# Expert weights in one 2 MB transfer per slot, with the middle layer's columns reordered

## The reference

```python
gu = xe @ w_gu[e]               # (32, 1024) @ (1024, 4096)
ga, up = split(gu, 2)           # 2048 columns each
y = (silu(ga) * up) @ w_down[e] # (32, 2048) @ (2048, 1024)
```

## Time and profile before

| | |
|---|---|
| time, three runs | 1652.12 us median (1649.69 to 1652.52) |
| span of the profiled execution | 1646.8 us (the profile gives its span alone; the timed runs lie 2.9 to 5.7 us above it) |
| busy share of the span | PE 79%, PEld 46%, DVE 22%, ACT 18%, POOL 4% |
| moved from memory | 499.67 MB, mean 304 GB/s |
| expert weights | 256 gate/up and 128 down transfers of 1 MB |

### The profile page before, as it was taken

One profiled execution on the slowest core, in us unless ns is written; L12 is line 12 of the kernel. 1 busy time (PEld: TensorE's weight loads), 2 busy tenths in 40 slices (PEclk: granted clock), 3 DMA queues, 4 the chain that ended last, 5 costly groups with the idle time before them and its releaser, 6 DMA issues.

```text
span 1646.8 us, 17841 instructions
## 1 busy us (share of the span) xinstructions
PE 1296.5 (79%) x7421; PEld 764.9 (46%) x7421; DVE 360.7 (22%) x552; ACT 289.1 (18%) x388; POOL 58.5 (4%) x37
## 2 busy tenths in 40 slices
PE   6999999999998989986566676577567576567665
PEld 5898778999776646532122122123122122122212
DVE  4653454555427142300000000000000000000001
ACT  4443443333344132200000000000000000000001
POOL 1000000000064000000000000000000000000000
PEclk9998999999998789987887877877887877777787
DMA  9553344555543008399999999999999999999996
GB/s 342 208 175 132 111 145 154 184 175 205 198 160 103 0 0 335 150 372 414 420 416 414 420 416 415 419 417 416 418 417 415 417 418 415 417 419 415 416 420 275
DMA packets 128030, 501.36 MB, mean 304 GB/s; under 512 B 7870, under 2 KB 32644, under 8 KB 94964
## 3 DMA queue, kind: packets, MB, share of 16 engines
q1 hardware_dynamic: 126628, 495.60, 76.1%
q0 software_dynamic: 1360, 5.15, 0.9%
HBM read 499.67 MB, written 1.05 MB: 304 GB/s over the span
## 4 chain that ended last, share of the span: by engine, by line
issue 58%; PE 35%; DVE 3%; ACT 1%; DMA 1%; SPq 0%; POOL 0%; POOLq 0%; ACTq 0%; DVEq 0%
PE psA L525 10%; PE psA L514 9%; PE psB L703 4%; PE psA L880 2%; DMA arena<-in_w_in_dram 1%; PE psA L574 1%; PE psA L919 1%; PE psB L681 1%; PE psA L712 1%; DVE arena L1602 1%; PE psB L630 1%; PE psB L631 0%; PE psB L838 0%; DVE arena L1639 0%; PE psB L787 0%
## 5 line engine op out<-in xcount | busy, mean ns | idle before, releaser
L987 PE MATMUL psB<-arena 128*32 128x512 f32 x2048 | 327.5, 772 | 238.2 <-DMA arena<-in_expert_w_gu_dram 237.5
L987 PEld LDWEIGHTS psB<-arena 128*32 128x32 f32 x2048 | 63.4, 125 | 476.8 <-DMA arena<-in_expert_w_gu_dram 356.2
L1405 DVE TENSOR_TENSOR split_r<-arena,split_r 128x2048 fp32r<-128x2048 f32 x65 | 148.9, 2291 | 183.2 <-ACT split_r L1056 183.2
L525 PE MATMUL psA<-hT_r,split_r 128*128 128x256 f32 x1536 | 185.9, 283 | 1.0 <-ACT hT_r L1065 1.0
L525 PEld LDWEIGHTS psA<-hT_r,split_r 128*128 128x128 f32 x1536 | 184.8, 192 | 2.0 <-ACT hT_r L1065 1.2
L1056 ACT CAST split_r<-arena 128x2048 fp32r<-128x2048 f32 x73 | 138.9, 1905 | 229.7 <-PE psA L525 113.3
L514 PE MATMUL psA<-split_r,hT_r 128*128 128x512 f32 x720 | 170.6, 397 | 5.2 <-ACT split_r L1056 3.0
L1312 ACT ACTIVATE arena<-psB 128x512 f32<-128x512 f32 x16 | 9.6, 597 | 878.3 <-PE psB L987 878.3
L1014 PE MATMUL psB<-arena,vs_b 128*32 128x512 f32 x1024 | 149.1, 737 | 16.3 <-DMA arena<-in_expert_w_down_dram 16.2
L514 PEld LDWEIGHTS psA<-split_r,hT_r 128*128 128x128 f32 x720 | 136.7, 192 | 36.3 <-issue 3.9
L964 PE MATMUL psB<-sb_b,xn_b 128*128 (+1 forms) x544 | 108.6, 377 | 12.3 <-ACT vs_b L1314 12.3
(11 more groups left out here) (313 smaller groups left out, 868.7 us busy)
## 6 DMA issues: line engine op xcount, KB each, us to landing
arena<-in_expert_w_gu_dram SPq DMA_DIRECT2D x256, 1024.0 KB, 25.5
arena<-in_expert_w_down_dram SPq DMA_DIRECT2D x128, 1024.0 KB, 20.6
arena<-in_w_in_dram SPq DMA_DIRECT2D x36, 1024.0 KB, 7.4
arena<-in_w_gate_dram SPq DMA_DIRECT2D x11, 1024.0 KB, 5.5
arena<-in_w_up_dram SPq DMA_DIRECT2D x11, 1024.0 KB, 8.1
arena<-in_w_down_dram SPq DMA_DIRECT2D x10, 1024.0 KB, 5.9
arena<-in_w_out_dram SPq DMA_DIRECT2D x8, 1024.0 KB, 6.3
arena<-in_ca_wkv_dram SPq DMA_DIRECT2D x4, 1024.0 KB, 6.4
```

What stands on the lines that cost most here:

```text
L525: ins = pe.matmul(psA[:, 2 * pair + b, f * TOK:(f + 1) * TOK], w[:, k, f * P:(f + 1) * P], x[:, k, :], start=(j == 0 and k == 0), stop=(j ...
L987: ins = pe.matmul(psB[32 * j:32 * j + 32, o, :], XC[:, k, :], w[:, o * EFF + j * NC:o * EFF + (j + 1) * NC], start=(k == 0), stop=(k == GU ...
L1405: v.tensor_tensor(W_LO[n % 2].rearrange("p (k n) -> p k n", **shape), view, W_HI[n % 2].bitcast(F32).rearrange("p (k n) -> p k n", **shape ...
```

## The change

One transfer now fills a slot, for both kinds of weights, and adds 16 to the slot's semaphore, so PE's wait counts 16 in place of 32. For gate/up each partition gets its whole row of 4096 columns. For down each partition gets four neighbouring rows of `w_down`, 16 KB that lie together in memory: partition p holds rows 512 j + 4 p + c. Block c of `HTE` must then hold the columns 4 p + c of the middle layer in place of 128 c + p; DVE's multiply writes `HE` in that order, reading `SL` and the bank straight on and writing with a stride of 128 elements.

```diff
                     s = x_slot[x_place(n)]
-                    for h in range(2):
-                        dst = s[:, h * HALF:(h + 1) * HALF]
-                        if j < GU_SLOTS:
-                            w = A["expert_w_gu_2"][0].rearrange("e k n -> (e k) n")
-                            src = w[bass.ds(e * (BODY * D) + (q * D + j * P), P), h * HALF:(h + 1) * HALF]
-                        else:
-                            w = A["expert_w_down_2"][0].rearrange("e (k p) n -> (e k) p n", p=P)
-                            src = w[bass.ds(e * (BODY * EFF // P) + (q * EFF // P + (j - GU_SLOTS) * 4 + 2 * h), 2), :, :].rearrange("k p n -> p k n")
-                            dst = dst.rearrange("p (k n) -> p k n", k=2)
-                        sp.dma_start(dst, src).then_inc(sig(f"expert_loaded{x_place(n)}"), 16)
+                    if j < GU_SLOTS:
+                        w = A["expert_w_gu_2"][0].rearrange("e k n -> (e k) n")
+                        src = w[bass.ds(e * (BODY * D) + (q * D + j * P), P), :]
+                    else:
+                        w = A["expert_w_down_2"][0].rearrange("e (r k) n -> (e r) (k n)", k=4)
+                        src = w[bass.ds(e * (BODY * EFF // 4) + (q * EFF // 4 + (j - GU_SLOTS) * P), P), :]
+                    sp.dma_start(s, src).then_inc(sig(f"expert_loaded{x_place(n)}"), 16)
...
-                        pe.wait_ge(sig(f"expert_loaded{x_place(n)}"), e * (32 * B_SLOTS // X_SLOTS) + 32 * (n // X_SLOTS + 1))
+                        pe.wait_ge(sig(f"expert_loaded{x_place(n)}"), e * (16 * B_SLOTS // X_SLOTS) + 16 * (n // X_SLOTS + 1))
...
-                    v.tensor_tensor(HE, SL, psB[:, 1, :], ALU.mult).then_inc(sig("e_he"), 1)
+                    v.tensor_tensor(HE.rearrange("p (c n) -> p n c", c=4), SL.rearrange("p (n c) -> p n c", c=4),
+                                    psB[:, 1, :].rearrange("p (n c) -> p n c", c=4), ALU.mult).then_inc(sig("e_he"), 1)
```

## The result

The changed kernel takes 1622.6 us (median of 4 runs, 1619.7 to 1628.9), the kernel before in the same comparison 1650.9 (4 runs, 1646.2 to 1652.5): ratio 0.9846, 95% interval 0.9815 to 0.9878, or 20 to 31 us saved. The profiled execution took 1621.85 us with a span of 1619.8, 2.05 us less; the 2.9 to 5.7 us at "Time and profile before" set the span beside other executions, and hold their spread too.

A forecast was written before the change was run, and what follows sets the result against it. The expert stage was taken as a DMA-bound stream of 2 MB slots. Saving 75 ns on 120 gate/up slots and 195 ns on 64 down slots gives 9.0 + 12.5 = 21.5 us, so 1652.1 becomes 1630.6 us, range 1622 to 1645.

The forecast's parts named there:

- What bounds the kernel: Expert stage: a DMA-bound stream of 2 MB slots, 4.990 us per gate/up slot and 5.110 us per down slot.
- (d): Expert stream: 120 gate/up and 64 down slots, 925.8 us, are the path; the change takes 21.5 us off.
- (a): Gate/up slots: 16 data packets per engine become 8, 60 ns less a slot.
- (b): Down slots: 32 data packets per engine become 8, 180 ns less a slot.
- the price of a packet: Weight transfers: each data packet costs an engine 7.5 ns, or 9.2 ns through the outer two points.
- (c): Each slot: one completion packet per engine in place of two, taken as 15 ns saved, between 0 and 85 ns.
- (e): SP's issues: 384 become 192; SP then waits for free slots, seven or eight on order, five while PE gathers; no cost.
- (g): DVE's multiply at line 1833, 687 ns: strided write taken to cost 0, ends 0 and +2.1 us; 0.9 us slack left.
- (h): Tail from PE's start on the last slot to the end of the span: keeps its 14.3 us.
- Rival A: Weight transfers: 16 KB runs are cut again into 8 KB packets; only 10.4 us saved, 1641.7 us; chance 0.10.
- B: Gate/up already at a memory or port limit, only down gains: 7.7 us saved, 1644.4 us; chance 0.11.
- C: Weight reads fall in step on the memory and the rate drops: 1663.8 us, or 1726 on both kinds; chance 0.06.

The follow-up runs named there:

- one_completion: Kernel before, with one transfer a slot but its old 8 KB and 4 KB runs, so half the completions; 1657.76 us, stream stretch 932.42 us against 932.63.
- order4: Changed kernel with at most four slots on order instead of eight, effective only in the first expert of each two; stream stretch 914.57 us against 909.07.
- mult3: Changed kernel with the reordered multiply done three times in a row in every expert; stream stretch 911.49 us against 909.07.
- pairs_plain: Changed kernel with 4 MB transfers filling two neighbouring slots (32 KB runs), most slots paired, reordering in PE's transposes; 1618.34 us, ratio to before 0.9827.
- order3: Changed kernel with at most three slots on order instead of eight, effective only in the first expert of each two; stream stretch 979.69 us, +70.6 us.

## Why the prediction was right, and which terms were off

**What bounds the kernel** and **(d), the stream as the path**: right. Its loss, 23.56 us, is the kernel's gain within the interval.

**(a), (b), the price of a packet**: mechanism right, size low by a fifth. I took 7.5 ns from the two kinds of slots and had 9.2 from the outer points in hand. Over five points it is 9.3; the step from 16 to 32 packets, on which I leaned, is the flattest of all (123 ns / 16 = 7.7), that from 8 to 16 the steepest (82/8 = 10.2). **(c), the completion**: 15 ns taken, nothing measured (one_completion). The packets were 4.5 us too cheap in the sum and the completions 2.8 too dear, so that 21.5 lies near is partly luck: with 9.3 and 0 the sum is 120 x 0.074 + 64 x 0.223 = 23.2 us; 23.56 measured. These are the terms that were mis-sized, and with them right the forecast would have been 1628.9 us. The other 6.3 us down to 1622.6 fit the spread of the first part, which the prediction did not count; that they come from it is not shown. Two slips change nothing: the earlier trace rows has slices at 414 too, and with 85 ns a completion the sum is 34.4 us, not 34.2. The Trainium skill's ceiling ("DMA: Bandwidth & Descriptors", "Where 436 GB/s comes from") agrees with the line's 4.831 us at no packets at all: 2.097 MB / 4.831 us = 434 GB/s beside its 435. What I put on completions by it belonged to the packets.

**(e), SP**: right. An issue now takes a third of a microsecond and SP waits for free slots:

```profile
L450 SPq DMA_DIRECT2D arena<-in_expert_w_gu_dram x128: 332/333/480, 621.8 to 1548.8; - x128
...
SPq L450 <- PE psB L984: 531.3, 124, 23.8
...
arena<-in_expert_w_gu_dram SPq DMA_DIRECT2D x128, 2048.0 KB, 35.4
```

35.4 us from issue to landing are 7.2 slots on order, as counted. "Five stay on order" was enough. The four of order4 count landed slots too: with the three that PE may hold, one is left on its way, and that is not enough when PE is slow.

**(g), the multiply**: the cost was not 0:

```profile
L1830 DVE TENSOR_TENSOR arena<-arena,psB 128x512 f32<-128x512 f32 x16 | 16.4, 1026 | 291.0 <-ACT arena L1309 291.0
```

+339 ns on 687, inside my ends. The row that I leaned on, line 1609, reads with a stride of two elements and writes straight on, so it could not show this. The cover held: 0.80 us of slack are left before the last down slot (0.9 forecast without that cost). Of them 0.3 us came by luck from PE, whose way from gathering to the 48th down matmul took 13.67 us where it took 13.97. mult3 shows what a dearer multiply would have done.

**(h)** right to 0.01 us. **Rival A** fell by the packet count (520 of 16 KB; over the whole span 128,030 packets became 83,997, one more gone than the 44,032 forecast). **B** fell: gate/up alone gained 82 ns a slot, and pairs_plain goes on past 428 GB/s. **C** fell: neither kind of slot lost by the pitch; no run here shows what the Trainium skill reports for other pitches.

## What to carry to other kernels

Where a stage is a stream that keeps the DMA engines full, take its time as bytes at the line's foot plus packets times their price, with packets counted per engine, and fit the price over as many run lengths as the trace has; two neighbouring points mislead. Longer contiguous runs per partition are bought by permuting the contraction, which costs little if the reordering falls where an engine has slack. Compare such kernels over the stretch that the change touches: in two profiles of the changed kernel it repeats within 0.1 us, where the whole time spreads by 10.

## What was not expected of the hardware

Completion packets cost nothing in a full stream (0.2 us over 184 slots with half of them gone). Inside gate/up the rate holds with three slots on order (4.90 us a slot in order3), and is lost only when the order runs dry. A run of 1 KB still moves 2.097/6.02 = 348 GB/s, one of 32 KB about 431 (4.868 us by the line, 430 over the window with some 16 KB slots in it). The multiply with a 512-byte write stride and grouped reads takes 1.5 times the plain one.
